# Triangular inversion as 32x32 tiles, the state product at level 4, GpSimd's operands between the level masks

## The chip, the cores and the metric

The kernel runs on one core of a Trainium2 chip. The metric is the device time of one execution in microseconds (us), the median of several runs.

## What is computed

Two transformer blocks in float32 on x[1024, 1024]: attention, convolution and MLP, then a layer with sparse attention and an RWKV-7 recurrence of 8 heads of 64. The change touches the recurrence alone:

```python
def rwkv7_step(state, inp):
    r_t, w_t, k_t, v_t, kk_t, a_t = inp
    sa = jnp.einsum('bhvk,bhk->bhv', state, -kk_t)
    state = (state * w_t[:, :, None, :] + sa[..., None] * (kk_t * a_t)[:, :, None, :]
             + v_t[..., None] * k_t[:, :, None, :])
    y = jnp.einsum('bhvk,bhk->bhv', state, r_t)
    return state, y
...
_, y = lax.scan(rwkv7_step, s0, (tm(rh), tm(wh), tm(kh), tm(vh), tm(kk), tm(ah)))
```

## The kernel before, in words

The 1024 steps are cut into 16 chunks of 64 (CHUNK, C). Inside a chunk the recurrence becomes matrix products and the inverse of a unit triangular 64x64 matrix for each head. Eight heads stand as four pairs m, each pair with head e = 0 on partitions 0 to 63 and e = 1 on 64 to 127. The inverse is built in LEVELS = 6 levels: level l joins diagonal blocks of size 2^l into blocks of twice the size. `off[..., l, m]` holds the matrix masked to the blocks that level l adds, `tt` the inverse so far, `gg` its transpose, `xx` a product in between. At each level TensorE makes X = off^T tt (`inv_x`), ScalarE copies X out of PSUM (L3479), TensorE makes the two W products (`inv_w`: one for tt, which the last level leaves out, one for gg), and VectorE adds them to tt (L3617) and gg (L3620). The four pairs are two groups i = 0, 1 (G[i]), each with banks x_bank[i] and w_bank[i] and semaphores of its own, so that one group's copies and adds run beside the other's products. `group_pairs` (L3265) makes one product of a group: 2 pairs x 2 heads, four matmuls of 64x64 by 64 columns. A float32 matmul leaves two records in the trace.

Each engine runs its own list in order and waits on semaphores; the order is written out by hand in the loops over chunks. TensorE's loop (from L3359), for chunk c: `state_part(c-1)` (L3262, the helper `pairs`), `inv_x(c,0)`, `turn` (transposes, L3283 and L3288), `solve(c-1)`, `inv_x(c,1)`, `value_part`, `inv_w(c,1)`; then for each l from 2 to 5 `inv_x(c,l)` and `inv_w(c,l)`, and between the two at l = 2 `y_part(c-1)` (L3343, L3347) and `state_product(c-1)` (L3355), at l = 3 `raw(c+1)` (L3013, the next chunk's raw products). After `inv_w` come `mean` (l = 3, chunks 8 to 11), `bonus` (l = 3, chunks 9 to 12) and `variance` (l = 4, chunks 9 to 12), each one 128x512 block (L3188).

VectorE's loop follows it: `combine` (L3585), gg and tt of level 0 (L3605, L3609), `zv` (L3611), then the adds of levels 1 to 5; after level 2's `next_state(c-1)` (L3590, L3591: the state plus the state product, times the decay), after level 3's `masked(c+1)` (L3026, two masks of the raw products). `state_part(c)` waits for next_state's semaphore s_ready. ScalarE copies the transposes (L3465, L3467), U (L3471), X, y (L3488), and at l = 4 the heads of the next chunk (L3031, L3032), which GpSimd waits for. GpSimd makes the six level masks of the next chunk (`chunk_levels`, L3038), then the operands of the one after (`chunk_operands`, L2997 to L3004), and in chunks 8 to 11 the bonus inputs (L3671, L3673), in 12 to 15 a low part of a weight piece (L404).

Of the kernel before, what the change touches and what calls it, by code (L numbers as in the profile page):

```python
# [3040 lines left out]
def rwkv_phase(k):  # L3041
# [101 lines left out]

    def bc(x, n=4):
        return x.unsqueeze(1).to_broadcast((x.shape[0], n, x.shape[1]))
# [38 lines left out]
    def _(pe):  # L3184
# [80 lines left out]
        def group_pairs(i, bank, at, lhs, rhs):  # L3265

            out = k.bank(bank)[:, at:at + 2 * CHUNK].rearrange("p (m c) -> p m c", m=2)
            for m in range(2):
                for e in range(2):
                    last = pe.matmul(out[rows(e), m], lhs(2 * i + m, e), rhs(2 * i + m, e), start=True, stop=True)  # L3270
            return last

# [23 lines left out]
        def inv_x(c, l):  # L3296

            pe.wait_ge(off_ready, LEVELS * c + l + 1)
            for i in range(2):
                if l == 0:  # L3300
                    last = group_pairs(i, x_bank[i], 0, lambda m, e: off[rows(e), c % 2, 0, m],
                                       lambda m, e: eye[rows(e)])
                else:
                    pe.wait_ge(t_ready[i], (LEVELS - 1) * c + l)
                    last = group_pairs(i, x_bank[i], 0, lambda m, e: off[rows(e), c % 2, l, m],
                                       lambda m, e: tt[rows(e), 0, m])
                last.then_inc(x_mm[i], 1)

        def inv_w(c, l):

            for i in range(2):
                pe.wait_ge(x_ready[i], (LEVELS - 1) * c + l)
                pe.wait_ge(g_ready[i], LEVELS * c + l)
                if l < LEVELS - 1:
                    group_pairs(i, w_bank[i], 0, lambda m, e: gg[rows(e), c % 2, m],
                                lambda m, e: xx[rows(e), l % 2, m])
                group_pairs(i, w_bank[i], 2 * CHUNK, lambda m, e: xx[rows(e), l % 2, m],
                            lambda m, e: gg[rows(e), c % 2, m]).then_inc(w_mm[i], 1)
# [40 lines left out]
        for c in range(C + 1):  # L3359
# [46 lines left out]
    def _(a):  # L3406
# [53 lines left out]
        for c in range(C + 1):  # L3460
# [11 lines left out]
            if c < C:  # L3472
                for l in range(1, LEVELS):
                    n = (LEVELS - 1) * c + l
                    for i in range(2):
# [3 lines left out]
                        a.copy(xx[:, l % 2, G[i]], half(x_bank[i], 0)).then_inc(x_ready[i], 1)  # L3479
# [38 lines left out]
    def _(v):  # L3518
# [80 lines left out]
        for c in range(C + 1):  # L3599
            if c >= 1:  # L3600
                combine(c - 1)
            if c < C:
# [9 lines left out]
                for l in range(1, LEVELS):  # L3612
                    for i in range(2):
# [6 lines left out]
                        v.tensor_tensor(gg[:, c % 2, G[i]], gg[:, c % 2, G[i]], half(w_bank[i], 2 * CHUNK),  # L3620
                                        ALU.add).then_inc(g_ready[i], 1)
                    if l == 2 and c >= 1:
                        next_state(c - 1)
# [35 lines left out]
    def _(g):  # L3659
# [26 lines left out]
        for c in range(C):  # L3686
            if 8 <= c < 12:
                bonus_in(c - 8)
            if c >= 12:
                pieces.lower(g, c - 11)  # L3690
            if c >= 2:
                g.wait_ge(x_mm[1], LEVELS * (c - 1))
            chunk_levels(k, g, chunk, c, range(0 if c else 1, LEVELS))
            if c + 1 < C:
                operands(c + 1)
# [168 lines left out]
```

## Time and profile before

| | us |
|---|---|
| median of 3 runs (lowest, highest) | 2630.66 (2630.11, 2630.99) |
| the profiled execution, its time | 2630.19 |
| the profiled execution, its span | 2628.2 |
| TensorE matmul busy | 2567.8 (98%), 19224 records |
| VectorE busy | 1561.6 (59%) |
| ScalarE busy | 1108.6 (42%) |
| GpSimd busy | 425.6 (16%) |

The time is the device time of the execution, the span reaches from the first to the last instruction in the trace. Busy is the sum of an engine's records; matmuls are pipelined and overlap, so 98% doesn't mean that the array streams all the time. A line number in a row is that of the kernel before; where a helper makes the instruction it is the helper's. The page's clock row shows the TensorE clock as granted, 1.00 for 2.4 GHz and 0.50 for 1.2 GHz.

### The profile page before, as it was taken

How to read it: one execution, taken by the hardware profiler on the slowest of the kernel's cores; microseconds unless marked ns; L12 is line 12 of the kernel's file. 1: busy time of each engine (PE TensorE's matmuls, PEld its weight loads, DVE VectorE, ACT ScalarE, POOL GpSimd, SP SyncE). 2: the span in 40 equal slices, each digit the busy share in tenths (PEclk: the TensorE clock that was granted, in tenths of full speed). 3: DMA queues.
4: the chain of work that ended last, by engine and by line, in shares of the span. 5: the costliest groups of instructions: out<-in, count | busy, mean ns of one | idle time of the engine just before them, and what ended most of it. 6: DMA issues, size and time to landing. Idle time of an engine off the chain costs nothing.

```text
span 2628.2 us, 46698 instructions
## 1 busy us (share of the span) xinstructions
PE 2567.8 (98%) x19224; PEld 2086.1 (79%) x19224; DVE 1561.6 (59%) x2521; ACT 1108.6 (42%) x2067; POOL 425.6 (16%) x381
## 2 busy tenths in 40 slices
PE   8999999999999999999999999999999999999998
PEld 6887777778778998899888777766776677788876
DVE  8765443436686665676546676355567646656754
ACT  3242233323355543556335554324445545344521
POOL 4421221100000000000000000111112100456644
PEclk9999999999999999999999999999999999999999
DMA  6753443134423454534534222631011253100032
GB/s 227 212 119 107 97 131 101 65 115 165 160 102 116 144 192 141 189 132 150 170 127 173 76 96 90 270 129 49 29 49 49 85 189 105 42 19 19 19 129 96
DMA packets 80754, 307.24 MB, mean 117 GB/s; under 512 B 7200, under 2 KB 8864, under 8 KB 62624
## 3 DMA queue, kind: packets, MB, share of 16 engines
q1 hardware_dynamic: 55984, 238.72, 25.9%
q0 software_dynamic: 12800, 33.56, 5.6%
q10 hardware_dynamic: 11760, 31.99, 3.2%
q8 instruction: 154, 2.52, 0.4%
q14 instruction: 56, 0.46, 0.1%
HBM read 268.32 MB, written 69.47 MB: 129 GB/s over the span
## 4 chain that ended last, share of the span: by engine, by line
PE 83%; DVE 9%; ACT 4%; issue 3%; DMA 1%; POOL 1%; DVEq 0%; ACTq 0%; SPq 0%; POOLq 0%
PE ps L425 46%; PE ps L3270 4%; PE ps L1258 4%; PE ps L1257 4%; PE ps L1259 4%; PE ps L2145 2%; PE ps L2191 2%; PE ps L2171 2%; PE ps L2072 2%; PE ps L609 2%; PE ps L635 1%; PE ps L2074 1%; PE ps L2073 1%; PE ps L624 1%; DVE parts L404 1%
## 5 line engine op out<-in xcount | busy, mean ns | idle before, releaser
L425 PE MATMUL ps<-parts,parts 128*128 128x512 f32 (+2 forms) x6456 | 1467.5, 387 | 15.9 <-DVE parts L804 8.8
L425 PEld LDWEIGHTS ps<-parts,parts 128*128 128x128 f32 x6456 | 1171.6, 188 | 299.7 <-issue 34.3
L404 DVE TENSOR_TENSOR parts<-ring,parts 128x1024 fp32r<-128x1024 f32 x180 | 220.8, 1238 | 174.7 <-ACT parts L381 166.3
L381 ACT CAST parts<-ring 128x1024 fp32r<-128x1024 f32 x183 | 188.7, 1044 | 116.9 <-DMA ring<-in_weights 62.1
L1257 PE MATMUL ps<-parts,parts 128*128 128x256 f32 x840 | 236.2, 281 | 1.3 <-ACT phase_data L1406 1.3
L1258 PE MATMUL ps<-parts,parts 128*128 128x256 f32 x840 | 236.1, 281 | 0.0
L1259 PE MATMUL ps<-parts,parts 128*128 128x256 f32 x840 | 236.0, 281 | 0.0
L404 POOL TENSOR_TENSOR parts<-ring,parts 128x1024 fp32r<-128x1024 f32 x62 | 153.2, 2472 | 423.1 <-DVE parts L381 423.0
L2552 POOL TENSOR_TENSOR phase_data<-phase_data,stream 128x512 f32<-128x512 f32 x12 | 17.2, 1436 | 1186.2 <-PE ps L2082 1186.2
L867 DVE TENSOR_TENSOR_SCAN stream<-stream 128x513 f32<-128x513 f32 (+3 forms) x96 | 95.2, 992 | 173.2 <-ACT stream L737 173.0
L1257 PEld LDWEIGHTS ps<-parts,parts 128*128 128x128 f32 x840 | 158.7, 189 | 2.4 <-ACT phase_data L1406 1.5
L1258 PEld LDWEIGHTS ps<-parts,parts 128*128 128x128 f32 x840 | 157.7, 188 | 0.8 <-issue 0.5
L1259 PEld LDWEIGHTS ps<-parts,parts 128*128 128x128 f32 x840 | 157.9, 188 | 0.0
L2270 ACT ACTIVATE stream<-stream,phase_data 128x640 f32<-128x640 f32 (+7 forms) x128 | 93.5, 731 | 84.8 <-DVE phase_data L2476 84.2
L1636 DVE TENSOR_TENSOR parts<-phase_data,parts 128x512 fp32r<-128x512 f32 (+1 forms) x111 | 78.1, 730 | 30.2 <-ACT parts L1565 11.0
L1647 DVE TENSOR_TENSOR parts<-ring,parts 128x1024 fp32r<-128x1024 f32 x60 | 72.5, 1220 | 33.1 <-ACT parts L1401 28.3
L3479 ACT COPY phase_data<-ps 128x128 f32<-128x128 f32 x160 | 40.1, 266 | 110.0 <-PE ps L3270 104.2
L2476 DVE CUSTOM_DVE_ANT_0 stream<-ps,phase_scratch 128x640 f32<-128x640 f32 (+4 forms) x96 | 54.4, 598 | 46.7 <-PE ps L2145 45.2
L1401 ACT CAST parts<-ring 128x1024 fp32r<-128x1024 f32 x60 | 63.1, 1051 | 44.3 <-PE ps L425 17.2
L1406 ACT COPY phase_data<-ps 128x256 f32<-128x256 f32 x120 | 44.8, 373 | 87.3 <-PE ps L1259 85.2
L1838 DVE TENSOR_TENSOR phase_data<-phase_data,ps 128x512 f32<-128x512 f32 x48 | 32.9, 686 | 81.8 <-PE ps L425 81.5
L3038 POOL TENSOR_TENSOR stream<-normed,phase_scratch 128x256 f32<-128x256 f32 x90 | 65.6, 763 | 91.1 <-ACT normed L3032 91.1
(391 smaller groups left out, 3761.6 us busy)
## 6 DMA issues: line engine op xcount, KB each, us to landing
ring<-in_weights SPq DMA_DIRECT2D x128, 1024.0 KB, 4.9
up_sums<-in_weights POOLq DMA_DIRECT2D x24, 1024.0 KB, 8.9
ring<-in_weights SPq DMA_DIRECT2D x32, 512.0 KB, 4.3
ring<-up_sums SPq DMA_DIRECT2D x30, 512.0 KB, 5.9
phase_data<-up_sums SPq DMA_DIRECT2D x60, 256.0 KB, 5.6
up_sums<-up_sums POOLq DMA_DIRECT2D x8, 1024.0 KB, 5.4
phase_data<-in_weights SPq DMA_DIRECT2D x30, 256.0 KB, 5.5
raw_keep<-phase_scratch SPq DMA_DIRECT2D x21, 256.0 KB, 2.4
```

The lines of the kernel that those rows point to most:

```text
L381: cast(self.hi(p), self.whole(p)).then_inc(self.k.hi_ready, 1)
L404: g.tensor_tensor(self.lo(p), self.whole(p), self.hi(p).bitcast(F32), ALU.subtract).then_inc(self.k.lo_ready, 1)
L425: last = pe.matmul(out, a, b, start=i == 0 and a is ah and b is bh, stop=i == len(pairs) - 1 and a is al)
L867: step(v.tensor_tensor_scan(back, back, back, 1.0, ALU.mult, ALU.min))
L1257: pe.matmul(out, hi, x_hi, start=first and t == 0, stop=False, skip_group_check=True)
L1258: pe.matmul(out, hi, x_lo, start=False, stop=False, skip_group_check=True)
L1259: last = pe.matmul(out, lo, x_hi, start=False, stop=t == 3, skip_group_check=True)
L1636: return v.tensor_tensor(lo, whole_, hi.bitcast(F32), ALU.subtract)
L1647: v.tensor_tensor(quad_lo(r, i), quad_whole(r, i), quad_hi(i).bitcast(F32), ALU.subtract).then_inc(weight_lo.sem, 1)
L2270: a.activation(tile, tile, ACT.Exp, bias=neg_max[:, n:n + 1], scale=-1.0, accum_out=sums[:, n:n + 1]).then_inc(e_ready, 1)
L3038: g.tensor_tensor(b.off[:, c % 2, l], b.mab(c), over_pairs(b.level[:, l]), ALU.mult).then_inc(k.off_ready, 1)
L3270: last = pe.matmul(out[rows(e), m], lhs(2 * i + m, e), rhs(2 * i + m, e), start=True, stop=True)
```

## The change

1. From chunk 1 on every product of the inversion at levels 0 to 4 goes as 32x32 tiles: `group_blocks` makes eight matmuls, one for each 32x32 diagonal block (2 pairs x 4 blocks), since up to level 4 nothing lies outside these blocks. At level 5 `group_corners` makes four, one for the off-diagonal 32x32 corner of each head. Chunk 0 keeps `group_pairs`, which writes the zeros that later chunks leave standing. Level 5 has its own columns in the banks (`x_at`, `w_at`).
2. `state_product(c-1)` moves from between X and W of level 2 to between X and W of level 4; `next_state` on VectorE moves from after level 2's adds to after level 4's; `mean` moves from level 3 to level 4.
3. GpSimd makes three level masks, then the next operands, then the other three masks; the bonus inputs and the weight pieces of a chunk come after its masks instead of before them.

```diff
@@ def rwkv_phase(k):
+    def x_at(l):
+        return 2 * CHUNK if l == LEVELS - 1 else 0
+    def w_at(l):
+        return 4 * CHUNK if l == LEVELS - 1 else 2 * CHUNK
...
+        def group_blocks(i, bank, at, lhs, rhs):
+            out = k.bank(bank)[:, at:at + 2 * CHUNK].rearrange("p (m c) -> p m c", m=2)
+            for m in range(2):
+                for q in range(4):
+                    here, side = slice(32 * q, 32 * q + 32), slice(32 * (q % 2), 32 * (q % 2) + 32)
+                    last = pe.matmul(out[here, m, side], lhs(2 * i + m, here, side), rhs(2 * i + m, here, side),
+                                     start=True, stop=True)
+            return last
+
+        def group_corners(i, bank, at, lhs, rhs, back):
...
+            for m in range(2):
+                for e in range(2):
+                    upper, lower = slice(64 * e, 64 * e + 32), slice(64 * e + 32, 64 * e + 64)
+                    left, right = slice(0, 32), slice(32, 64)
+                    if back:
+                        last = pe.matmul(out[upper, m, right], lhs(2 * i + m, lower, left), rhs(2 * i + m, lower, right),
+                                         start=True, stop=True)
+                    else:
+                        last = pe.matmul(out[lower, m, left], lhs(2 * i + m, upper, right), rhs(2 * i + m, upper, left),
+                                         start=True, stop=True)
+            return last
+
+        def group_of(c, l, back=False):
+            if c == 0:
+                return group_pairs
+            if l < LEVELS - 1:
+                return group_blocks
+            return lambda i, bank, at, lhs, rhs: group_corners(i, bank, at, lhs, rhs, back)
...
@@ TensorE's loop
                     if l == 2 and c >= 1:
                         y_part(c - 1)
-                        state_product(c - 1)
                     if l == 3 and c + 1 < C:
                         raw(c + 1)
+                    if l == 4 and c >= 1:
+                        state_product(c - 1)
                     inv_w(c, l)
-                    if l == 3 and 8 <= c < 12:
+                    if l == 4 and 8 <= c < 12:
                         mean(c - 8)
...
@@ VectorE's loop
-                    if l == 2 and c >= 1:
+                    if l == 4 and c >= 1:
                         next_state(c - 1)
...
@@ GpSimd's loop
         for c in range(C):
-            if 8 <= c < 12:
-                bonus_in(c - 8)
-            if c >= 12:
-                pieces.lower(g, c - 11)
             if c >= 2:
                 g.wait_ge(x_mm[1], LEVELS * (c - 1))
-            chunk_levels(k, g, chunk, c, range(0 if c else 1, LEVELS))
+            chunk_levels(k, g, chunk, c, range(0 if c else 1, 3))
             if c + 1 < C:
                 operands(c + 1)
+            chunk_levels(k, g, chunk, c, range(3, LEVELS))
+            if 8 <= c < 12:
+                bonus_in(c - 8)
+            if c >= 12:
+                pieces.lower(g, c - 11)
```

How the change moves instructions, at the places of the prediction's steps. TensorE before, in a chunk, from X of level 2 to W of level 3 (L3270 is the inversion, L3343 and L3347 the y part, L3355 the state product, L3013 the raw products; the number at the end of a row counts matmuls):

```order
L3270 MATMUL ps<-stream 64x64 x8
L3343 MATMUL ps<-normed,phase_data 64x64 x8
L3347 MATMUL ps<-normed 64x64 x8
L3355 MATMUL ps<-normed 64x64 x8
L3270 MATMUL ps<-phase_data,stream 64x64 x4
L3270 MATMUL ps<-stream,phase_data 64x64 x4
L3270 MATMUL ps<-phase_data,stream 64x64 x4
L3270 MATMUL ps<-stream,phase_data 64x64 x4
L3270 MATMUL ps<-stream 64x64 x8
L3013 MATMUL ps<-phase_scratch,normed 128x128 x8
```

TensorE now, from X of level 4 to the next chunk's level 0 (L3288 is `group_blocks`, L3303 and L3300 `group_corners`, L3397 the state product, L3270 now `pairs`, here the state part):

```order
L3288 MATMUL ps<-stream 32x32 x16
L3397 MATMUL ps<-normed 64x64 x8
L3288 MATMUL ps<-phase_data,stream 32x32 x8
L3288 MATMUL ps<-stream,phase_data 32x32 x8
L3288 MATMUL ps<-phase_data,stream 32x32 x8
L3288 MATMUL ps<-stream,phase_data 32x32 x8
L3303 MATMUL ps<-stream 32x32 x8
L3300 MATMUL ps<-stream,phase_data 32x32 x8
L3270 MATMUL ps<-phase_data,normed 64x64 x8
L3288 MATMUL ps<-phase_scratch,stream 32x32 x16
```

The state product stands between X and W of level 4 now, a product of the inversion has twice the matmuls at levels 0 to 4 and as many as before at level 5, and the shape of the tiles changes 14 times in a chunk for 6 before.

VectorE now, from the masks of the raw products (L3026) over the adds of level 4 (L3660, L3663) and next_state (L3633, L3634) to level 5's adds:

```order
L3026 TENSOR_TENSOR normed<-ps,phase_scratch 128x512 x2
L3660 TENSOR_TENSOR stream<-stream,ps 128x128
L3663 TENSOR_TENSOR stream<-stream,ps 128x128
L3660 TENSOR_TENSOR stream<-stream,ps 128x128
L3663 TENSOR_TENSOR stream<-stream,ps 128x128
L3633 TENSOR_TENSOR phase_data<-phase_data,ps 128x256
L3634 TENSOR_TENSOR phase_data<-phase_data,phase_scratch 128x256
L3663 TENSOR_TENSOR stream<-stream,ps 128x128 x2
```

Before, the pair L3590, L3591 stood between the adds of level 2 and those of level 3.

## Rows read from the trace of the kernel before

**Rows 1.** The page: the chain that ended last, by line.
```profile
PE ps L425 46%; PE ps L3270 4%; PE ps L1258 4%; PE ps L1257 4%; PE ps L1259 4%; PE ps L2145 2%; PE ps L2191 2%; PE ps L2171 2%; PE ps L2072 2%; PE ps L609 2%; PE ps L635 1%; PE ps L2074 1%; PE ps L2073 1%; PE ps L624 1%; DVE parts L404 1%
```
**Rows 2.** Stretches: chunks 1 to 7, 9 to 11: busy by engine, clock, DMA.
```profile
2269.49:2375.63 106.14, 102.14 (x2527) 91.03 (x2525) 59.84 (x197) 43.39 (x140) 59.01 (x87) 1.00 0.04 13
...
2391.72:2445.06 53.34, 51.58 (x1104) 41.23 (x1102) 34.27 (x98) 23.43 (x69) 34.29 (x42) 1.00 0.07 23
```
**Rows 3.** Timeline, TensorE, chunk 6: start us, us, engine, line, operation, tiles, records.
```profile
2345.30 0.63 PE L3262 MATMUL ps<-phase_data,normed 64*64 64x64 f32 x16
...
2345.77 0.63 PE L3270 MATMUL ps<-phase_scratch,stream 64*64 64x64 f32 x16
...
2349.34 0.45 PE L3270 MATMUL ps<-phase_data,stream 64*64 64x64 f32 x8 [0.25 <-ACT phase_data L3479]
...
2350.51 0.82 PE L3270 MATMUL ps<-stream 64*64 64x64 f32 x16
...
2351.72 0.69 PE L3347 MATMUL ps<-normed 128*64 128x64 f32 x16
...
2352.24 0.64 PE L3355 MATMUL ps<-normed 128*64 128x64 f32 x16
...
2352.81 0.45 PE L3270 MATMUL ps<-phase_data,stream 64*64 64x64 f32 x8
...
2354.72 1.16 PE L3013 MATMUL ps<-normed 64*128 64x128 f32 x16
...
2355.82 0.45 PE L3270 MATMUL ps<-phase_data,stream 64*64 64x64 f32 x8
...
2356.98 0.82 PE L3270 MATMUL ps<-stream 64*64 64x64 f32 x16
...
2357.78 0.45 PE L3270 MATMUL ps<-phase_data,stream 64*64 64x64 f32 x8
...
2359.04 0.75 PE L3270 MATMUL ps<-stream 64*64 64x64 f32 x16
...
2360.47 0.63 PE L3262 MATMUL ps<-phase_data,phase_scratch 64*64 64x64 f32 x16
```
**Rows 4.** Timeline, TensorE, starts within 0.06 us, and at a seam.
```profile
2348.27 0.27 PE L3262 MATMUL ps<-normed 64*64 64x64 f32 x1
...
2350.51 0.27 PE L3270 MATMUL ps<-stream 64*64 64x64 f32 x2
```
**Rows 5.** Timeline, VectorE, chunk 6: adds, state update, masks of raw products.
```profile
2354.00 0.29 DVE L3617 TENSOR_TENSOR stream<-stream,ps 128x128 f32<-128x128 f32 x1
...
2354.41 0.42 DVE L3590 TENSOR_TENSOR phase_data<-phase_data,ps 128x256 f32<-128x256 f32 x1
...
2354.86 0.42 DVE L3591 TENSOR_TENSOR phase_data<-phase_data,phase_scratch 128x256 f32<-128x256 f32 x1
...
2357.41 1.28 DVE L3026 TENSOR_TENSOR normed<-ps,phase_scratch 128x512 f32<-128x512 f32 x2
```
**Rows 6.** Timeline, VectorE and GpSimd, chunk 15.
```profile
2502.89 1.27 POOL L3671 TENSOR_TENSOR phase_data<-phase_data 128x512 f32<-128x512 f32 x1
...
2502.94 1.50 DVE L3591 TENSOR_TENSOR phase_data<-phase_data,phase_scratch 128x256 f32<-128x256 f32 x1
```
**Rows 7.** Timeline, GpSimd, chunk 6: level masks, last operand; TensorE, chunk 0.
```profile
2344.61 4.25 POOL L3038 TENSOR_TENSOR stream<-normed,phase_scratch 128x256 f32<-128x256 f32 x6 [7.04 <-ACT normed L3032]
...
2351.99 0.74 POOL L3004 TENSOR_TENSOR normed<-phase_data,normed 128x256 f32<-128x256 f32 x1
...
2262.99 1.16 PE L3013 MATMUL ps<-normed 64*128 64x128 f32 x16 [0.52 <-POOL normed L3004]
```
**Rows 8.** Stretches: a fall of the clock, and a gap without one.
```profile
1751.20:1754.60 3.40, 1.31 (x13) 1.07 (x12) 1.72 (x2) 2.27 (x4) 0.00 (x0) 1.00 1.00 366
...
1754.60:1758.00 3.40, 3.40 (x9) 2.65 (x8) 2.30 (x5) 0.00 (x0) 0.95 (x1) 0.50 0.41 159
...
2502.20:2505.60 3.40, 2.03 (x55) 1.74 (x54) 3.37 (x9) 0.81 (x3) 3.30 (x3) 1.00 0.00 0
```

More of the change, by code:

```diff
@@ L3269, in group_pairs @@
                 for e in range(2):
-                    last = pe.matmul(out[rows(e), m], lhs(2 * i + m, e), rhs(2 * i + m, e), start=True, stop=True)
-            return last
+                    last = pe.matmul(out[rows(e), m], lhs(2 * i + m, rows(e), slice(0, CHUNK)),
+                                     rhs(2 * i + m, rows(e), slice(0, CHUNK)), start=True, stop=True)
+            return last
+        def group_blocks(i, bank, at, lhs, rhs):
[7 more added lines that the diff above has]
+        def group_corners(i, bank, at, lhs, rhs, back):
+            out = k.bank(bank)[:, at:at + 2 * CHUNK].rearrange("p (m c) -> p m c", m=2)
+            for m in range(2):
[15 more added lines that the diff above has]
+            return lambda i, bank, at, lhs, rhs: group_corners(i, bank, at, lhs, rhs, back)
         def raw(c):
@@ L3298, in inv_x @@
             pe.wait_ge(off_ready, LEVELS * c + l + 1)
+            multiply = group_of(c, l)
             for i in range(2):
                 if l == 0:
-                    last = group_pairs(i, x_bank[i], 0, lambda m, e: off[rows(e), c % 2, 0, m],
-                                       lambda m, e: eye[rows(e)])
+                    last = multiply(i, x_bank[i], 0, lambda m, r, s: off[r, c % 2, 0, m, s], lambda m, r, s: eye[r, s])
                 else:
                     pe.wait_ge(t_ready[i], (LEVELS - 1) * c + l)
-                    last = group_pairs(i, x_bank[i], 0, lambda m, e: off[rows(e), c % 2, l, m],
-                                       lambda m, e: tt[rows(e), 0, m])
+                    last = multiply(i, x_bank[i], x_at(l), lambda m, r, s: off[r, c % 2, l, m, s],
+                                    lambda m, r, s: tt[r, 0, m, s])
                 last.then_inc(x_mm[i], 1)
         def inv_w(c, l):
+            multiply = group_of(c, l, True)
             for i in range(2):
@@ L3314, in inv_w @@
                 if l < LEVELS - 1:
[L3315 to L3318, printed above, removed]
+                    multiply(i, w_bank[i], 0, lambda m, r, s: gg[r, c % 2, m, s], lambda m, r, s: xx[r, l % 2, m, s])
+                multiply(i, w_bank[i], w_at(l), lambda m, r, s: xx[r, l % 2, m, s],
+                         lambda m, r, s: gg[r, c % 2, m, s]).then_inc(w_mm[i], 1)
         def state_part(c):
@@ L3478, in _ @@
                             a.wait_ge(w_mm[i], n - 2)
-                        a.copy(xx[:, l % 2, G[i]], half(x_bank[i], 0)).then_inc(x_ready[i], 1)
+                        a.copy(xx[:, l % 2, G[i]], half(x_bank[i], x_at(l))).then_inc(x_ready[i], 1)
                     if l == 2 and c == 0:
@@ L3686, in _ @@
         for c in range(C):
+            if c >= 2:
+                g.wait_ge(x_mm[1], LEVELS * (c - 1))
+            chunk_levels(k, g, chunk, c, range(0 if c else 1, 3))
+            if c + 1 < C:
+                operands(c + 1)
+            chunk_levels(k, g, chunk, c, range(3, LEVELS))
             if 8 <= c < 12:
```

6 lines of the change are left out of this document (1 added, 5 removed).

## The prediction

> **What bounds the kernel now.** I read the page first (its chain and its lines), then the stretches chunk by chunk, then TensorE's timeline of one chunk, and last what VectorE and GpSimd do there. The chain gives 46% of the span to the matmuls of the projections and 4% to L3270, the small products of the inversion [rows 1]. The change touches that stage alone: chunks 0 to 15, 2255.5 to 2508.8 us, some 253 of 2628.2 us. Chunks 1 to 7 take 106.14 us together, 15.16 each; chunks 9 to 11 take 53.34, 17.78 each. The clock is at 1.00 and the DMA share under a tenth in both [rows 2]. So what counts is a chunk's own chain, the wait that ends last at each level.
>
> One chunk on TensorE, from one state part (L3262, eight matmuls, which leave sixteen records) to the next [rows 3]:
> - a, 4.04 us, 2345.30 to 2349.34: state part, level 0, transposes, solve, level 1, value part. It ends on ScalarE's copy of X, not on TensorE: the row at 2349.34 says so.
> - b, 1.17, W products of level 1 to X products of level 2; f and h, 1.16 and 1.26, the same from level 3 to 4 and from 4 to 5. VectorE adds in between.
> - c, 2.30, X of level 2 to W of level 2, with the y part (its last block is L3347) and the state product (L3355) between; g, 0.80, the same of level 4 with nothing between.
> - d and e, 3.01, W of level 2 over X of level 3 and the raw products (L3013) to W of level 3.
> - i, 1.43, X of level 5 over its W to the next state part.
>
> How fast the array takes small products: 16 records of 64x64 start from 2345.30 to 2345.77, 0.058 us for two [rows 3]. Two records start within 0.06 us of each other, and a record of the value part (L3262) starts at 2348.27 in the middle of level 1's (L3270), on an idle tile [rows 4]. So tiles run beside each other, each takes a record in 0.058 us, and a later product need not wait for a busy tile. The 16 records of L3013, twice as many columns, last 1.16 us in all, 0.27 of it the last one's own time (that of [rows 4]): 0.11 for two, twice as long for twice the columns. A product on the next shape of tile costs more: L3347, first after a change of shape, needs 0.52 to the next block where 0.47 is usual, and from L3355 to the next 64x64 block it is 0.57, 0.10 more than its own 0.47 [rows 3]. A change of shape costs 0.15 us where nothing hides it.
>
> **The change, step by step.** *Blocks.* A product of a pair group has 4 matmuls of 64x64 now and 8 of 32x32 afterwards, on four diagonal tiles. Four rounds of 0.058 (0.23 us) become four rounds of half the columns. No row has a tile of 32. I scale by columns, as 128 against 64 scale: 0.032 with the fixed part of some 0.005, so 0.13. Ends: 0.032 below, 0.058 above, if the record got no shorter. I take 0.032, since the two widths that the rows show lie on that line. A record's own tail shrinks by some 0.03.
>
> Here the rows meet a rule. The two records that start together belong to e = 0 and 1, rows 0 to 63 and 64 to 127, and both write the same bank [rows 4]. The Trainium skill (TensorEngine Tiling (Array Packing), Restrictions and Gotchas) says that different row tiles cannot access the same PSUM bank simultaneously. By that rule the sixteen records would go one after another, 0.51 us for 0.23 now, and each chunk would lose more than 5 us. The trace disagrees for two row tiles.
>
> - b, d, f: W of a group is two products, 0.47 to 0.26; with the tail 0.24 less, three times: 0.72. h has that too, and loses the 0.10 that the masks (L3026, 1.28 us from 2357.41 [rows 5]) make level 4's adds late, since the state product now puts these adds later: 0.34.
> - a: level 0 saves 0.21 and a change of shape before it costs 0.15: 0.06. What level 1 saves, and three more changes of shape there, lie beside ScalarE's copies, which still end a. Were ScalarE not late there, the three would cost 0.45.
> - e: X saves 0.14 (its second group starts 0.35 after the first, VectorE's adds, and then takes 0.13).
> - c: X 0.12 and tail 0.02, the state product leaves with 0.47, and a change of shape from 32x32 to the y part adds 0.15: 0.46 less.
>
> *State product in level 4.* g becomes X 0.48, change 0.15, product 0.47, change 0.12 (a shorter refill for 32 columns): 1.22 for 0.80, costing 0.41. It comes from c, where it was fully on the path too, so the move itself pays little. VectorE's state update moves with it, behind level 4's adds: L3590, 0.45 to L3591's start, then L3591, 0.42; a group's two adds take 0.41 [rows 5]. The next state part waits for it, and behind that wait stands all of the next chunk. From X of level 5 (T) the adds end at T+0.38, the update at T+1.25, and the state part starts at T+1.31. Here GpSimd comes in: its masks of the next chunk start just after the heads' copies, beside L3591. In chunk 15 L3591 took 1.50 instead of 0.42, and ended 0.28 after the GpSimd instruction that ran when it started (1.27 from 2502.89) [rows 6]. A mask is 0.71 (six take 4.25 [rows 7]), so the delay is between 0 and 0.6; the heads' copies end at about T+0.4, the mask runs to T+1.2 and L3591 is held past it, so I take 0.25: T+1.55. i is 1.43 now: 0.12 lost; the change of shape before the state part lies behind this wait.
>
> *GpSimd's operands between masks.* Operands take 2352.73 - 2348.86 = 3.9 us [rows 7]. Level 3's mask is there 3 x 0.71 + 3.9 + 0.71 = 6.7 us after the first mask starts, 0.7 before the chunk: 6.0 into it. X of level 3 comes after a, b, c and d, 3.98 + 0.93 + 1.84 + 0.92 = 7.7. That cover is 1.7 us; without it every level from 3 on would wait. In chunk 0 the raw products stood 0.52 for the operands [rows 7], which goes, since only two masks are ahead of them now.
>
> Plain chunk: 0.06 + 0.72 + 0.34 + 0.46 + 0.14 - 0.41 - 0.12 = 1.19 us, 13.97 for 15.16. Seven of them: 8.3. In chunks 8 to 11 the mean (one 128x512 block) moves from level 3 to 4 and waits for the state update: it starts at T+1.56 where X of level 5 would have started at T, and stands before it in TensorE's queue, so level 5 waits too. The 0.42 by which the state part waited goes, 1.14 is lost, and almost nothing is left of 1.19: 0.3 for all four. Chunks 12 to 15 count as plain, 4.8; chunk 15's own stall [rows 6] I leave as it is, since GpSimd's last work sits beside the update again. With chunk 0: 8.3 + 0.3 + 4.8 + 0.5 = **13.9 us**. Against the profiled execution: span 2628.2 to 2614.3, time 2630.19 to 2616.3. The median lies 0.47 above that execution, so 2616.8.
>
> **Rivals.**
> *Small records get no shorter (slower).* Each round stays at 0.058, twice the records on twice the tiles. a then loses 0.15, c gains 0.30, g loses 0.55, h gains 0.10, i loses 0.12: -0.42 per plain chunk, -1.56 in chunks 8 to 11, so 0.5 - 11 x 0.42 - 4 x 1.56 = -10.4: 2641.1. It decides from a round of 0.047 on, where the gain is zero. For it: no row has tiles of 32. Against it: rounds of 0.058 and 0.11 for 64 and 128. The Trainium skill has a rule for it (TensorEngine Tiling (Array Packing), Instruction Overhead): a matmul with few columns takes as long as one with 60. 0.12.
> *A round in between*, 0.045, four tiles fed too slowly: by proportion 13.9 - 24.3 x 0.5 = 1.8 us gained, up to 5 where waits hide part; about 2627. 0.08.
> *The clock falls.* It fell to 0.50 from 1754.6 for a whole row, after one in which TensorE was busy 1.31 of 3.40 us, and stayed at 1.00 where it was busy 2.03 of 3.40 [rows 8]. In the changed levels TensorE streams for 0.76 of 1.6 us per level, its tails aside, so less than in any stretch of this stage now. A fall costs 1.0 to 1.7 us of doubled streaming; 14 falls cancel the gain, one to a chunk is 2632 to 2642. 0.06.
> *GpSimd does not catch the update.* 0.25 back in eleven chunks, 0.45 in four: 4.5 more, 2612.3. For it: the two are within some tenths of each other. 0.12.
> My forecast: 0.62, its own range 2611 to 2622.
>
> **How the numbers follow.** The range 2609 to 2629 takes in the forecast, the uncaught update and the round in between, 0.82. Measured against no change, 0.2% (5.3 us) is what can be told. Faster: 0.62 + 0.12 and a part of the in-between case, 0.77. Same: its rest, 0.05. Slower: 0.18, the first rival and the clock.
>
> **What would show it.** Right: products of 16 records within 0.13 us; W to X 0.92 for 1.16; the gap in front of the state part ended by VectorE's second state instruction, not TensorE; chunks of 14.0, and 17.7 for 9 to 11; ScalarE still ending a; the clock at 1.00. Wrong: rounds of 0.058; a clock of 0.50 in the levels; X of level 3 waiting for GpSimd; L3591's successor at 0.42 everywhere.

## The result, and the profile after

Median 2684.5 us of 4 runs (2681.4 to 2689.3), against 2630.4 of 4 runs of the kernel before on the same chip: 1.0207 of its time, 95% interval 1.0191 to 1.0223. The change costs 54 us where I had forecast a gain of 14, and the time lies far outside my range. The profiled execution has a span of 2687.4 us and a time of 2689.3, 59 us more than the span before. Functions that moved in the file have new line numbers: L3288 is the 32x32 block product, L3303 and L3300 are the corners, L3270 is the old `pairs`, L3325 the first transpose of a chunk, L3397 the state product, L3633 or L3634 the second instruction of the state update.

The first lines of the page and its chain, for [rows 1]:

```profile
span 2687.4 us, 52948 instructions
PE 2585.1 (96%) x22344; PEld 2088.1 (78%) x22344; DVE 1562.0 (58%) x2521; ACT 1109.2 (41%) x2067; POOL 425.1 (16%) x381
...
q8 instruction: 178, 2.92, 0.4%
...
PE 83%; DVE 8%; issue 4%; ACT 3%; DMA 1%; POOL 0%; DVEq 0%; SPq 0%; ACTq 0%; POOLq 0%
```

TensorE has 3120 matmul records and as many weight loads more than before, and the queue that brings instructions moved 178 packets, 2.92 MB, where the page before has 154 and 2.52 MB. The packets are of 16 KB, and the 0.40 MB more for 6240 instructions more makes 64 bytes for each, 256 to a packet. The other engines do what they did.

The stretches, for [rows 2]. I cut them from one first transpose (L3325) to the next now: chunk 0, chunks 1 to 7, 8 to 11, 12 to 14.

```profile
2256.54:2270.26 13.72, 12.53 (x316) 10.89 (x313) 8.17 (x28) 5.91 (x19) 8.39 (x14) 1.00 0.24 80
2270.26:2399.84 129.58, 106.84 (x3986) 90.29 (x3977) 58.44 (x198) 43.81 (x140) 59.32 (x89) 0.79 0.04 12
2399.84:2491.00 91.16, 71.60 (x2299) 52.07 (x2293) 45.13 (x128) 30.80 (x92) 48.76 (x62) 0.85 0.05 15
2491.00:2549.47 58.47, 48.48 (x1708) 40.59 (x1709) 36.12 (x99) 25.54 (x69) 28.43 (x33) 0.77 0.08 22
```

The same cuts of the kernel before:

```profile
2270.52:2376.66 106.14, 102.14 (x2525) 91.03 (x2521) 59.84 (x198) 43.39 (x140) 59.01 (x87) 1.00 0.04 13
2376.66:2446.50 69.84, 67.30 (x1464) 54.54 (x1461) 44.27 (x129) 31.27 (x92) 46.40 (x58) 1.00 0.06 18
2446.50:2494.42 47.92, 45.37 (x1084) 39.26 (x1085) 34.53 (x99) 25.61 (x69) 31.70 (x38) 1.00 0.09 25
```

So 23.4, 21.3 and 10.6 us were lost, 55 of the 59. Two things in the rows are new: a mean clock of 0.77 to 0.85, and TensorE idle for 23 of 129.6 us. The clock is 0.50 (1.2 GHz) or 1.00, so a mean of 0.79 is 54 us at 0.50 in chunks 1 to 7. The length of a chunk does not follow the clock, though: chunk 1, with 4.0 us at 0.50, takes 17.88 us, chunk 4, with 8.1, takes 17.59.

TensorE's timeline in chunk 3 at full clock, for [rows 3]. "issue" means that the engine waited for nothing that the profile shows:

```profile
2308.88 0.33 PE L3288 MATMUL ps<-phase_data,stream 32*32 32x32 f32 x16 [0.31 <-ACT phase_data L3522]
2309.03 0.31 PE L3288 MATMUL ps<-stream,phase_data 32*32 32x32 f32 x16
...
2309.84 0.63 PE L3288 MATMUL ps<-stream 32*32 32x32 f32 x32 [0.21 <-DVE stream L3660]
...
2311.78 0.25 PE L3288 MATMUL ps<-stream,phase_data 32*32 32x32 f32 x9
2312.56 0.26 PE L3288 MATMUL ps<-stream,phase_data 32*32 32x32 f32 x7 [0.53 <-issue]
...
2315.24 0.26 PE L3288 MATMUL ps<-phase_data,stream 32*32 32x32 f32 x6
2316.62 0.28 PE L3288 MATMUL ps<-phase_data,stream 32*32 32x32 f32 x10 [1.13 <-issue]
```

The products are as short as forecast: the second block of 16 records starts 0.15 us after the first, the four of a level's W take 0.13 each otherwise, and W to X is 0.96. But in the middle of a product, after its ninth and after its sixth record, TensorE stops for 0.5 to 1.1 us. I counted the instructions on its queue (matmuls, weight loads, waits) from one such gap (over 0.5 us from one instruction's start to the next, and no semaphore waited for) to the next: between 2279 and 2436 us there are 19 gaps, and all 18 distances are 256 or a multiple of it, 512 to 1024. Each gap ends 2.2 to 2.8 us after an instruction packet started. The one that ends at 2316.62 does so 2.35 us after the packet of 2314.27. So what TensorE waits for there is its instructions.

The instruction queue in chunks 1 to 7, first after, then before: 31 packets in 129.6 us, one in 4.2; 20 in 106.1, one in 5.3.

```profile
q8 instruction: 31, 0.51, 1.6%
```

```profile
q8 instruction: 20, 0.33, 1.3%
```

Theories for the experiments. **F**: TensorE gets no more than some 64 instructions a us over a chunk; a chunk has 1155 of them on its queue now, 738 before (the expectations say 1148, and call chunks of 17.6 to 18.1 us full clock that had 4 to 11 us at 0.50 each). **A**: the clock falls since the small tiles keep the array streaming for too small a part of the time. **M**: the moves of state product, update, mean and operands cost it. F and A may act together: a stall is also a time without streaming.

### The profile page after: what moved, and what is told of

It is laid out like the page before. It is cut to its first block, busy times and chain, and to the rows that moved or that the text cites. A ratio compares the mean times of both kernels' runs of the same rounds, so it can differ in the third digit from the quotient of the medians.

```text
span 2687.4 us, 52948 instructions
## 1 busy us (share of the span) xinstructions
PE 2585.1 (96%) x22344; PEld 2088.1 (78%) x22344; DVE 1562.0 (58%) x2521; ACT 1109.2 (41%) x2067; POOL 425.1 (16%) x381
## 3 DMA queue, kind: packets, MB, share of 16 engines
q8 instruction: 178, 2.92, 0.4%
## 4 chain that ended last, share of the span: by engine, by line
PE 83%; DVE 8%; issue 4%; ACT 3%; DMA 1%; POOL 0%; DVEq 0%; SPq 0%; ACTq 0%; POOLq 0%
PE ps L425 45%; PE ps L1258 4%; PE ps L1257 4%; PE ps L1259 4%; PE ps L3288 3%; PE ps L2145 2%; PE ps L2191 2%; PE ps L2171 2%; PE ps L2072 2%; PE ps L609 2%; PE ps L635 1%; PE ps L2073 1%; PE ps L2074 1%; PE ps L624 1%; PE ps L3270 1%
## 5 line engine op out<-in xcount | busy, mean ns | idle before, releaser
L3660 DVE TENSOR_TENSOR stream<-stream,ps 128x128 f32<-128x128 f32 x128 | 36.5, 285 | 101.3 <-PE ps L3288 78.6
```

## The experiments

Each ratio is against the kernel before, run beside the experiment on the same chip.

### The parts of the change

*moves_only*: everything of the change but the tiles.

```diff
         def group_of(c, l, back=False):
-            if c == 0:
-                return group_pairs
-            if l < LEVELS - 1:
-                return group_blocks
+            return group_pairs
```

> The change with its 64x64 products kept at every level; only the state product, its update, the mean and GpSimd's operands move. Theory F (TensorE is starved of instructions by the many small records) and theory A (the clock falls since small tiles stream too little) both say that the moves are nearly neutral: 2628 to 2636 us, clock at 1.00 in the stage, gaps without a releaser at the size of the kernel before. Theory M (the moves cost it: state product, update and masks on the path) says 2655 or more.

Measured: 2642.0 us (2639.8 to 2643.8), 1.0046 of the time before (1.0031 to 1.0061). That lies between the two ranges: the moves cost 12 us. They cost next to nothing in chunks 1 to 7:

```profile
2271.84:2378.42 106.58, 103.41 (x2524) 91.43 (x2521) 59.73 (x198) 43.82 (x140) 58.35 (x85) 1.00 0.04 13
2378.42:2458.96 80.54, 70.97 (x1465) 55.45 (x1461) 46.56 (x130) 31.23 (x92) 51.18 (x67) 0.96 0.05 16
2458.96:2509.49 50.53, 46.31 (x1085) 39.80 (x1085) 38.48 (x95) 25.84 (x69) 26.83 (x30) 1.00 0.08 24
```

Chunks 8 to 11 take 10.7 us more than before, 12 to 14 another 2.6. In chunk 8 the trace names what the mean (L3196) waits for, the second half of VectorE's update (L3633):

```profile
2392.62 1.10 PE L3196 MATMUL ps<-phase_data,constants 128*128 128x512 f32 x2 [1.50 <-DVE phase_data L3633]
```

In chunk 9 that update ends at 2411.40, and TensorE's next work behind it is the mean again:

```profile
2409.99 0.41 DVE L3632 TENSOR_TENSOR phase_data<-phase_data,ps 128x256 f32<-128x256 f32 x1
2410.44 0.96 DVE L3633 TENSOR_TENSOR phase_data<-phase_data,phase_scratch 128x256 f32<-128x256 f32 x1
```

```profile
2411.50 3.52 PE L3196 MATMUL ps<-phase_data,constants 128*128 128x512 f32 x4 [1.96 <-issue]
```

```profile
2409.02 2.10 POOL L3038 TENSOR_TENSOR stream<-normed,phase_scratch 128x256 f32<-128x256 f32 x3 [6.35 <-ACT normed L3032]
```

TensorE is idle for 1.96 us, level 5 stands behind the mean, and in this chunk and in chunk 11 the clock falls as that gap ends, so that the four records of mean and variance take 3.52 us. The update's second half takes 0.96 for 0.42 [rows 5] beside GpSimd's masks, as in [rows 6].

*moves_early*: moves_only, with state product, update and mean in their old places from chunk 8 on.

```diff
                     if l == 2 and c >= 1:
                         y_part(c - 1)
+                        if c >= 8:
+                            state_product(c - 1)
...
-                    if l == 4 and c >= 1:
+                    if l == 4 and 1 <= c < 8:
                         state_product(c - 1)
...
-                    if l == 4 and 8 <= c < 12:
+                    if l == 3 and 8 <= c < 12:
                         mean(c - 8)
...
-                    if l == 4 and c >= 1:
+                    if l == (4 if c < 8 else 2) and c >= 1:
                         next_state(c - 1)
```

> moves_only with the state product, its update and the mean back in their old places from chunk 8 on; GpSimd's operands between the masks in every chunk. If the 12 us of moves_only are the mean that waits for the late state update (chunks 8 to 11 took 80.5 us for 69.8), these chunks are back at 70 and the time is within 2 us of the kernel before. If it is GpSimd's order, they stay at 75 or more and the time at 2636 or more.

Measured: 2628.9 us, 0.9996 (0.9988 to 1.0005). Chunks 8 to 11 are back at 69.84 us, chunks 12 to 14 at 48.19 for 50.53, chunk 0 is 13.80 for 14.40. So the 10.7 us of chunks 8 to 11 come from the late update with the mean behind it. The 2.6 of chunks 12 to 14, where no mean stands, go with the late update too: there the state part (L3270) waits for L3633, by 0.2 to 0.3 us in two of the three chunks; the rest of the 2.6 I did not trace. GpSimd's order costs nothing that can be measured here.

*blocks_only*: the tiles without any move.

```diff
-            chunk_levels(k, g, chunk, c, range(0 if c else 1, 3))
+            chunk_levels(k, g, chunk, c, range(0 if c else 1, LEVELS))
             if c + 1 < C:
                 operands(c + 1)
-            chunk_levels(k, g, chunk, c, range(3, LEVELS))
...
-                    if l == 4 and c >= 1:
+                    if l == 2 and c >= 1:
                         state_product(c - 1)
```

The state's update is back in level 2 and the mean in level 3 likewise.

> The 32x32 tiles without the moves. F and A: nearly the whole loss is here, 2670 to 2695 us, with the gaps of 0.7 to 1.3 us and the clock at 0.50 for about 130 us. M: 2612 to 2625, faster than the kernel before.

Measured: 2669.7 us (2666.9 to 2674.5), 1.0148 (1.0131 to 1.0165). The tiles cost 39 us, the moves 12; together 51 of the 54. M falls as the cause of most of the loss.

```profile
2268.73:2401.66 132.93, 106.99 (x3986) 90.66 (x3977) 58.34 (x198) 43.48 (x140) 60.65 (x90) 0.80 0.04 12
```

*corners_only*: the kernel before, with 32x32 tiles in level 5 alone, which adds no instruction.

```diff
         def group_of(c, l, back=False):
-            if c == 0:
-                return group_pairs
-            if l < LEVELS - 1:
-                return group_blocks
+            if c == 0 or l < LEVELS - 1:
+                return group_pairs
             return lambda i, bank, at, lhs, rhs: group_corners(i, bank, at, lhs, rhs, back)
```

> The kernel before, with level 5 alone on 32x32 tiles from chunk 1 on: no instruction more, and the other levels on 64x64. F and A: about as before, 2626 to 2632; level 5 saves 0.1 us in each of two products on the path and pays up to two changes of shape of 0.15, and the clock stays at 1.00.

Measured: 2629.4 us, 0.9995 (0.9986 to 1.0005), 15.11 us a plain chunk for 15.16, the clock at 1.00. Small tiles as such do no harm.

### Instructions or streaming

*half_blocks*: the changed kernel with every second block product left out. What it computes is no longer the inverse; only its time is of use.

```diff
             for m in range(2):
-                for q in range(4):
+                for q in (0, 2):
```

> The changed kernel with every second block product of levels 0 to 4 left out (half of the inversion's work there), so a chunk has as many TensorE instructions as in the kernel before, still on 32x32 tiles. F: the long gaps go and, since they are what lets the clock fall, the clock stays at 1.00; some 13 us a chunk, 2600 to 2615 us. A: even less is streamed, so the clock is at 0.50 for at least as long as in the changed kernel; 2640 to 2680 us, though the gaps are gone.

Measured: 2689.5 us (2680.3 to 2691.3), 1.0220 (1.0202 to 1.0238), as slow as the changed kernel (2681.4 to 2689.3) though it does half of the blocks. Chunk 1, chunk 5, and chunks 1 to 7:

```profile
2270.30:2284.23 13.93, 12.12 (x366) 10.19 (x361) 8.58 (x29) 6.17 (x20) 8.34 (x13) 1.00 0.01 3
2337.60:2357.08 19.48, 19.17 (x364) 16.68 (x360) 8.06 (x29) 6.27 (x20) 8.11 (x13) 0.50 0.16 57
2270.30:2394.80 124.50, 118.98 (x2527) 102.54 (x2521) 57.57 (x198) 43.68 (x140) 58.45 (x88) 0.63 0.03 11
```

Chunk 1 is the chunk that I had forecast, 13.93 us for 13.97, without a gap in a product. Then the clock falls with no stall before it: chunks 1 to 7 have no gap over 0.5 us that a semaphore does not explain. It is at 0.50 for 93 of 124.5 us, and a chunk is 5.55 us longer then. A holds, and F is not the whole. Here is also the only place where my stretches can be read one by one:

```profile
2273.32 0.31 PE L3288 MATMUL ps<-phase_data,stream 32*32 32x32 f32 x8 [0.33 <-ACT phase_data L3522]
2273.46 0.29 PE L3288 MATMUL ps<-stream,phase_data 32*32 32x32 f32 x8
...
2274.24 0.62 PE L3288 MATMUL ps<-stream 32*32 32x32 f32 x16 [0.23 <-DVE stream L3660]
...
2276.01 0.31 PE L3288 MATMUL ps<-phase_data,stream 32*32 32x32 f32 x8
...
2278.57 0.31 PE L3288 MATMUL ps<-phase_data,stream 32*32 32x32 f32 x8
...
2279.49 0.62 PE L3288 MATMUL ps<-stream 32*32 32x32 f32 x16 [0.23 <-DVE stream L3660]
...
2280.65 0.31 PE L3288 MATMUL ps<-phase_data,stream 32*32 32x32 f32 x8
...
2283.25 0.68 PE L3270 MATMUL ps<-phase_data,normed 64*64 64x64 f32 x16 [0.38 <-DVE phase_data L3634]
```

*half_fill*: the same, with something to stream in the waits of chunks 1 to 7.

```diff
+        def fill():
+            for q in range(4):
+                here = slice(32 * q, 32 * q + 32)
+                pe.matmul(four(5, P)[here], ident[here, here], ident[here].unsqueeze(1).to_broadcast((32, 4, P)),
+                          start=True, stop=True)
...
                 last.then_inc(x_mm[i], 1)
+            if 1 <= c < 8 and 1 <= l < LEVELS - 1:
+                fill()
```

> half_blocks with something for the array to stream in the waits: in chunks 1 to 7, after the X products of levels 1 to 4, one round of 512 columns on the four diagonal 32x32 tiles into an idle PSUM bank (0.43 us, beside ScalarE's copies, 16 instructions a level). In half_blocks these chunks took 13.93 to 19.49 us, 124.5 together, at a clock of 0.50 for most of it. Theory A (too little streamed lets the clock fall): the clock stays at 1.00, about 14 us a chunk, 98 to 103 for the seven. If streaming has nothing to do with it: 124 or more, and the fill itself would add up to 3 us a chunk at 0.50.

Measured: 2681.1 us, 1.0194 (1.0179 to 1.0209). Chunks 1 to 7, and chunk 5:

```profile
2269.77:2390.99 121.22, 113.02 (x2750) 76.16 (x2745) 54.88 (x198) 43.80 (x140) 58.50 (x88) 0.97 0.04 12
2339.95:2356.75 16.80, 15.64 (x398) 10.48 (x393) 7.69 (x29) 6.26 (x20) 8.15 (x13) 1.00 0.19 66
```

The clock is back, 0.97 for 0.63, and that speaks for A. The time is not: the fill takes 0.72 us a level on the path, four times, more than the wait has room for (16.80 for 13.93), so my number of 14 was wrong and the two effects nearly cancel. The 0.43 us that I had reckoned for the fill is one record's (0.44 to the next start on its tile). A float32 matmul leaves two on each tile, and the eight records of a fill (L3311), the last six of them here, run from 2341.80 to the next product at 2342.82:

```profile
2341.86 1.03 PE L3311 MATMUL ps<-constants 32*32 32x512 f32 x6
```

*after_fill*: the same fill in the changed kernel.

> The same fill in the changed kernel, nothing left out of it. A: the clock stays at 1.00 in chunks 1 to 7. F (TensorE's instructions arrive no faster than about 64 a us, since the changed kernel's chunks at full clock took 17.6 to 18.1 us for 1148 instructions, which is 15.5 ns each): the chunk is then 1148 + 64 = 1212 instructions, 18.8 us, 131 for seven, no gain over the 129.6 of the changed kernel. A alone, without a limit on instructions: about 14 us a chunk, 98 to 103.

Measured: 2688.3 us, 1.0220 (1.0203 to 1.0237).

```profile
2268.94:2405.11 136.17, 120.75 (x4210) 81.89 (x4200) 55.71 (x197) 43.37 (x140) 57.84 (x86) 0.94 0.04 12
```

The clock is at 0.94 for 0.79, and the seven chunks take 136, not 98: F said 131 with no gain over 129.6. Chunks 1 and 4, without any fall, take 17.7 and 18.9 us for 1218 instructions, 14.5 and 15.6 ns each. The fill's own cost on the path (0.72 a level above) would explain 16.8 at the most. The gaps at multiples of 256 instructions are still there, ten over 0.5 us, so the clock alone does not explain the changed kernel.

*repeats*: the changed kernel with level 0's product issued five times in chunks 1 to 7.

```diff
                 if l == 0:
+                    for _ in range(4 if 1 <= c < 8 else 0):
+                        multiply(i, x_bank[i], 0, lambda m, r, s: off[r, c % 2, 0, m, s], lambda m, r, s: eye[r, s])
                     last = multiply(i, x_bank[i], 0, lambda m, r, s: off[r, c % 2, 0, m, s], lambda m, r, s: eye[r, s])
```

> The changed kernel with the level-0 product of each group issued five times instead of once in chunks 1 to 7: 256 more TensorE instructions a chunk, 1.04 us more of the array's time by 0.13 us a product. F: 1404 x 15.5 ns = 21.8 us a chunk. Limit by the array alone: at most 1.1 us more than the changed kernel's chunk, 19.0 at full clock.

Measured: 2710.6 us, 1.0305 (1.0289 to 1.0320). From the transposes of chunk 1 to those of chunk 7 (six chunks, each with the repeats of the next) it is 22.2 us a chunk, 20.9 to 23.5. F's 21.8 fits the size, but the mean clock is 0.75, so the time alone does not settle it. The packets come one in 4.0 us (38 in 152.9), hardly faster than the one in 4.2 of the changed kernel, with 22% more instructions to bring. And TensorE stops 15 times for over 0.5 us with no semaphore to wait for, each time a multiple of 256 instructions behind the last. That fits F, and no limit of the array.

```profile
q8 instruction: 38, 0.62, 1.7%
```

*split_columns*: moves_only, each 64x64 product issued as two of 32 columns.

```diff
             for m in range(2):
-                for e in range(2):
-                    last = pe.matmul(out[rows(e), m], lhs(2 * i + m, rows(e), slice(0, CHUNK)),
-                                     rhs(2 * i + m, rows(e), slice(0, CHUNK)), start=True, stop=True)
+                for s in (slice(0, 32), slice(32, 64)):
+                    for e in range(2):
+                        last = pe.matmul(out[rows(e), m, s], lhs(2 * i + m, rows(e), slice(0, CHUNK)),
+                                         rhs(2 * i + m, rows(e), s), start=True, stop=True)
```

> The moves_only order, each 64x64 product of the inversion issued as two of 32 columns: as many TensorE instructions as the changed kernel, as many columns streamed as the kernel before. F: gaps of 0.7 to 1.3 us about every 256 instructions as in the changed kernel, 2655 to 2690 us. A: streaming as before, so the clock stays at 1.00 and the time is within 5 us of moves_only.

Measured: 2753.0 us (2719.4 to 2778.8), 1.0426 (1.0359 to 1.0492). The worst of all, and neither theory's way:

```profile
2275.21:2417.77 142.56, 142.56 (x4204) 136.95 (x4201) 57.81 (x197) 43.88 (x140) 58.22 (x86) 1.00 0.04 12
```

```profile
2298.59 0.66 PE L3279 MATMUL ps<-phase_data,stream 64*64 64x32 f32 x16
2299.07 0.63 PE L3279 MATMUL ps<-stream,phase_data 64*64 64x32 f32 x16
```

A product of 16 records of 32 columns takes 0.47 us, 8 of 64 columns take 0.23 [rows 3]: a record on a 64x64 tile costs the same with half the columns. So in chunks 1 to 7 the clock stays at 1.00, no gap stands in a product, and they are slow by doubled rounds alone, 20.37 us a chunk. (From chunk 8 on the clock fell as well.) It tells F and A nothing, as I had not allowed for that, except a bound: 1218 instructions in 20.37 us, 60 a us, still come in time when they are taken evenly.

### How many blocks pay

*w23*, *w234*, *w1234*: corners_only, with the W products of these levels on 32x32 tiles.

```diff
+            if c >= 1 and back and l in (2, 3):
+                return group_blocks
             if c == 0 or l < LEVELS - 1:
                 return group_pairs
```

> corners_only with the W products of levels 2 and 3 on 32x32 tiles as well: 128 more TensorE instructions a chunk, 866. F (no more than one instruction in 15.5 ns): 866 x 15.5 = 13.4 us a chunk, below the chain, so no stall; two levels save 0.24 us each, 14.6 us for 15.11, about 2623 in all. A (little streaming lets the clock fall): some falls, at most to the time of corners_only, 2629, or above if they are many.

> The same with levels 2, 3 and 4: 930 instructions, F gives 14.4 us at least and the chain 14.4, so 14.4 to 14.9 us a chunk and 2620 to 2627 in all at full clock. A: more falls than w23.

> The same with levels 1 to 4: 994 instructions. F: 15.4 us a chunk though the chain would allow 14.2, with the first long gaps that nothing releases; 2631 or more. Without a limit on instructions: 14.2 at full clock, 2617.

Measured: w23 2627.9 us, 0.9991 (0.9983 to 1.0000); w234 2637.0, 1.0031 (1.0019 to 1.0043); w1234 2646.0, 1.0056 (1.0043 to 1.0068). Chunks 1 to 7 of the three in turn:

```profile
2271.99:2378.44 106.45, 98.21 (x2972) 86.31 (x2969) 59.89 (x198) 43.47 (x140) 59.21 (x87) 0.97 0.04 14
2301.34:2315.91 14.57, 13.40 (x429) 11.85 (x425) 8.27 (x30) 6.16 (x20) 7.83 (x13) 1.00 0.02 5
```

```profile
2269.58:2380.71 111.13, 99.07 (x3197) 86.96 (x3193) 59.85 (x198) 43.22 (x140) 59.69 (x88) 0.93 0.04 13
```

```profile
2269.80:2386.91 117.11, 104.13 (x3419) 91.55 (x3417) 59.57 (x198) 43.51 (x140) 60.39 (x89) 0.85 0.04 13
```

| kernel | instructions a chunk | chunks 1 to 7, us | shortest chunk | mean clock | stops |
|---|---|---|---|---|---|
| corners_only | 738 | 105.7 | 15.10 | 1.00 | 0 |
| w23 | 866 | 106.5 | 14.56 | 0.97 | 1 |
| w234 | 930 | 111.1 | 15.02 | 0.93 | 3 |
| w1234 | 994 | 117.1 | 15.09 | 0.85 | 6 |
| changed kernel | 1155 | 129.6 | 17.59 | 0.79 | 14 |

Stops are gaps in chunks 1 to 7 of over 0.5 us with no semaphore waited for. Within each trace they all lie multiples of 256 instructions apart, and each ends 2.2 to 2.8 us after an instruction packet started. The kernel before, moves_only, half_blocks and split_columns have none there.

w23's shortest chunk is what the shorter products promise, 14.56 for 15.10. From 930 instructions on, even the shortest chunk no longer follows the chain (14.4 and 14.2 were due; w234 was to take 2620 to 2627 us in all), with more stops and more time at 0.50. F's floor of 15.5 ns is not sharp: w1234 has one chunk at 15.2 ns an instruction.

*w23_fill*: w23, with 128 columns on two 64x64 tiles in the wait after W of levels 2 and 3. *w23_gp*: w23 with GpSimd's operands between the masks in chunks 0 to 7. *w23_gp_fill*: both.

```diff
+            if c >= 1 and l in (2, 3):
+                for e in range(2):
+                    pe.matmul(k.bank(x_bank[0])[rows(e), 4 * CHUNK:6 * CHUNK], ident[rows(e), rows(e)], ident[rows(e)],
+                              start=True, stop=True)
```

```diff
-            chunk_levels(k, g, chunk, c, range(0 if c else 1, LEVELS))
+            first = range(0 if c else 1, 3 if c < 8 else LEVELS)
+            chunk_levels(k, g, chunk, c, first)
             if c + 1 < C:
                 operands(c + 1)
+            if c < 8:
+                chunk_levels(k, g, chunk, c, range(3, LEVELS))
```

> w23 with one round of 128 columns on two 64x64 tiles after the W products of levels 2 and 3, into an idle bank, in the wait for VectorE (8 instructions a level). If falls of the clock take the rest of w23's gain and more streaming holds the clock: no fall in the stage, chunks of 14.6, 2622 to 2625. If the fill does not fit in the wait, up to 0.1 us a level more, 2625 to 2628. If a fall does not depend on what is streamed: the falls of w23 stay, 2628 or more.

> w23 with GpSimd's operands between the level masks in chunks 0 to 7. Chunk 0 loses its wait for the operands, 14.41 to 13.8, the other chunks as in w23: 0.6 us less than w23, about 2627.3. If the masks of levels 3 and 4 came late instead, chunks 1 to 7 would be longer than 14.6 at full clock.

> Both together: 0.6 us below w23_fill, 2621 to 2625, if they add up; the best of all versions then.

Measured: w23_fill 2624.9 us, 0.9982 (0.9973 to 0.9991); w23_gp 2627.5, 0.9991 (0.9982 to 1.0000); w23_gp_fill 2625.3, 0.9982 (0.9973 to 0.9991). Chunks 1 to 7 of w23_fill, and what is left of the trouble in its chunk 4:

```profile
2271.57:2376.11 104.54, 98.49 (x3028) 86.62 (x3024) 59.44 (x198) 43.27 (x140) 58.91 (x87) 1.00 0.04 14
```

```profile
2322.51 0.33 PE L3288 MATMUL ps<-phase_data,stream 32*32 32x32 f32 x15
2323.43 0.18 PE L3288 MATMUL ps<-phase_data,stream 32*32 32x32 f32 x1 [0.60 <-issue]
...
2326.61 0.35 PE L3278 MATMUL ps<-stream 64*64 64x64 f32 x5
2328.01 0.39 PE L3278 MATMUL ps<-stream 64*64 64x64 f32 x6 [1.04 <-issue]
```

w23_fill beats both kernels, by 5.7 us against the kernel before. Its chunks are 14.6 to 14.8 but for chunk 4, 16.47, with two gaps 256 instructions apart: what it still loses there is the supply of instructions. w23_gp, with 866 instructions a chunk and the clock at 1.00 throughout chunks 1 to 7, has four such stops, and its chunks 2 and 5 take 16.7 and 16.6 us. That the fill also holds the clock fits the profiled run (no fall in the stage, where w23's has some), but w23_gp's profiled run had none either, so single runs do not show it. The medians of w23 and w23_fill are 3.0 us apart, with intervals that overlap: the fill's part in the gain stays open. GpSimd's order took chunk 0 from 14.41 to 13.80, and its 0.6 us cannot be seen in the medians.

## Why the prediction was wrong

Two steps failed. First, the change is costed as if an instruction were free once the array can take it. "A product of a pair group has 4 matmuls of 64x64 now and 8 of 32x32 afterwards" counted them, and the cost step then went only by rounds; that a chunk has 1155 instructions instead of 738, in bursts of 250 a us (a record and its load in 0.008 us, where a burst of 64x64 products has 68 a us), had no term at all, and was no rival either. What the runs showed: stops at multiples of 256 instructions, and a packet in 4.0 to 4.2 us on average at best. In chunks 1 to 7 of the changed kernel the 14 stops add up to 17 us, on top of the 97.8 forecast.

Second, *The clock falls* had the right mechanism and the wrong size. I gave it 0.06, one fall a chunk and 1.0 to 1.7 us a fall. half_blocks shows a chunk at 0.50 to be 19.48 us instead of 13.93, so a microsecond at 0.50 costs 0.28, a fall of 6.8 us 1.9, and a fall lasted up to 55 us, 54 us of 129.6 in all in the changed kernel. The rule that I took the case from, [rows 8], had one row of each kind, and "less than in any stretch of this stage now" was the warning that I priced too low.

The two losses add up. The third column is the chain as forecast (97.8 is 7 x 13.97, w234 and w1234 by their expectations, w23 by its shortest chunk, half_blocks by its chunk 1); stops is the sum of the stops of the table above, and clock the time at 0.50 (54.2, 93.2, 34.9, 15.3 and 6.8 us) at 0.28 a microsecond, the price that half_blocks gave:

| kernel | measured, us | chain | stops | clock | sum |
|---|---|---|---|---|---|
| changed kernel | 129.6 | 97.8 | 17.2 | 15.2 | 130.2 |
| half_blocks | 124.5 | 97.5 | 0 | 26.1 | 123.6 |
| w1234 | 117.1 | 99.4 | 5.3 | 9.8 | 114.5 |
| w234 | 111.1 | 100.8 | 3.9 | 4.3 | 109.0 |
| w23 | 106.5 | 101.9 | 1.7 | 1.9 | 105.5 |

The sums miss the measured time by 1 to 3 us; shorter gaps at the same places, 1 to 2 us in each of the last three kernels, are part of that. So of the 32 us over the forecast in chunks 1 to 7, the supply of instructions took some 17 and the clock some 15. How far a stop brings on a fall of the clock is open: w23's fall begins 1.2 us behind its one stop of 1.7 us, w23_gp has one of 2.1 us with no fall, and half_blocks fell with no stop.

Third and smaller: chunks 8 to 11. I had the wait (mean behind the update, level 5 behind the mean) and took 1.14 us a chunk for it, against savings of 1.19. moves_only, where those savings are not there, lost 10.7 us in the four chunks, 2.7 each, with TensorE idle 1.96 us; the variance stands behind the mean as well, and two falls of the clock double their time. Chunks 12 to 14 were costed as plain; moves_only lost another 2.6 us there.

What held, by my stretches, in half_blocks' chunk 1 at full clock (its blocks take the same 0.13 to 0.15 a product; here on two tiles):

| stretch | forecast | measured |
|---|---|---|
| a | 3.98 | 3.95 |
| b, f, h | 0.93, 0.92, 0.92 | 0.92, 0.92, 0.92 |
| c | 1.84 | 1.77 |
| d and e | 2.63 | 2.56 |
| g | 1.21 | 1.16 |
| i | 1.55 | 1.68 |

So 0.032 for a round on four tiles, the changes of shape, ScalarE as the end of a, the update caught by GpSimd (i is 0.13 more than forecast), the cover of GpSimd's reorder and chunk 0 (13.72 for 14.40, 0.5 forecast) were right, and the rivals *Small records get no shorter* and *A round in between* were wrong. Four row tiles wrote one bank at once, 16 records in 0.13 to 0.15 us, as two had [rows 4]: the section Restrictions and Gotchas of the Trainium skill's TensorEngine Tiling (Array Packing) does not hold here. Its Instruction Overhead rule, that few columns cost as much as about 60, agrees with split_columns: on a 64x64 tile 32 columns do cost as much as 64. On a 32x32 tile it does not hold: there a round of 32 columns takes 0.032 us and not 0.058.

## What to carry to other kernels

Before splitting small matmuls into smaller ones, count TensorE's instructions over the length of the chain they stand in, and look in the trace how often its instruction packets come: once the count over the time nears what the packets have ever brought, shorter products end in gaps that nothing releases. Here the first such gaps came with 866 instructions in chunks of 14.6 us, 59 a us, where the packets brought 64 a us at best. Ask also what the array still streams when its products get shorter: the waits between them stay, and the clock can fall and take more than the products gave. Cut where both leave room, one or two levels at a time, and give the longest chunk a look, not only the shortest.

## What the runs showed of the hardware that I had not expected

- TensorE stops for 0.5 to 2.7 us, at multiples of 256 instructions, until 2.2 to 2.8 us after a 16 KB instruction packet started. The mean rate alone does not tell when: 14 stops with 1155 instructions in 18.5 us, four with 866 in 15.3 (w23_gp), none with 1218 taken evenly over 20.4 (split_columns).
- Records on two 64x64 tiles start 0.029 us apart, with 64 columns and with 32. My scaling of the round by streamed columns gave the right number for 32x32 tiles, but for a reason that split_columns refutes. Nor do the columns of the weights alone set it: w23_fill's four records of 128 columns on two 64x64 tiles take 0.28 us, where four of 64 take 0.12. What fits these rows, at full clock, is the larger of the two counts, streamed columns or columns of the weights: 32, 64, 128 and 512 go with 0.032, 0.058, 0.11 to 0.14 and 0.44 us a round.

```profile
2308.35 0.44 PE L3363 MATMUL ps<-constants 64*64 64x128 f32 x4
2308.63 0.75 PE L3278 MATMUL ps<-stream 64*64 64x64 f32 x16
```

- The clock fell with 738 instructions a chunk and no gap in any product (half_blocks), and came back with two records of 512 columns on each tile, some 0.9 us, in four waits a chunk (half_fill).
- In split_columns the clock stayed at 0.50 for 51 us from chunk 8 on, so chunk 9 took 43.2 us; what kept it down there is open.
